# A two-layer encoder on one core: the output product in eight pieces, its weights chunk by chunk, two PSUM banks for transposed weights and three for scores, x and result on two queues

## The reference

```
diff heads (8): s = einsum('mbhqd,mbhkd->mbhqk', q, k) * scale + bias      # two maps m of 512 keys
                a = softmax(s);  w = a[0] - lam * a[1]
                o = rms_norm(w @ v, norm_g) * (1 - lam_init)
near heads (8): s = q @ k_window * scale + bias (masked);  o = softmax(s) @ v_window   # 256 keys
h = concat(o_diff, o_na) @ w_out                    # (512 x 1024) @ (1024 x 1024)
x = layer_norm(alpha * x + h, ln1_g, ln1_b)
f = PEER(x)                                         # routing, 16384 experts, 8 heads x top 16
x = layer_norm(alpha * x + f, ln2_g, ln2_b)
```

## Time and profile before

| | us |
|---|---|
| timed executions (3) | 3433.43, 3438.35, 3439.59 |
| median | 3438.35 |
| the profiled execution's own time | 3430.17 |
| its span, first to last instruction | 3428.4 |
| setup, to the first instruction of project | 0 to 19.1 |
| attend of the first layer | 172 to 402 |
| attend of the second layer | 1870 to 2102 |
| from the last vector instruction to the end | 3410.0 to 3428.4 |

### The profile page before, as it was taken

The page is one execution under the profiler, slowest core; times in us unless marked ns, Lnnn a source line. Parts: engine busy times, 40 slices in busy tenths (PEclk is TensorE's granted clock), DMA queues, the critical chain, the costliest instruction groups (busy, mean ns, idle before and its releaser), DMA issues. The chain is left out here.

```text
span 3428.4 us, 48751 instructions
## 1 busy us (share of the span) xinstructions
PE 3166.2 (92%) x16726; PEld 2801.7 (82%) x16726; DVE 2477.6 (72%) x5112; ACT 1233.9 (36%) x1756; POOL 1086.5 (32%) x684
## 2 busy tenths in 40 slices
PE   7978799899899999999889787998999999999996
PEld 6855489899899999988677555898988999999885
DVE  3165298899688888778732563898986888787786
ACT  2355233344333333333323552333443333332332
POOL 0030046500255545433200200573003555454331
PEclk9989899999999999999989998999999999999998
DMA  7541224455899999889675312243649999898995
GB/s 256 139 126 38 100 82 158 156 205 214 332 341 351 336 330 338 322 307 350 223 267 126 105 56 91 91 169 137 237 196 364 349 351 341 317 339 289 335 355 185
DMA packets 334536, 806.11 MB, mean 235 GB/s; under 512 B 38928, under 2 KB 195088, under 8 KB 299824
## 3 DMA queue, kind: packets, MB, share of 16 engines
q1 hardware_dynamic: 258576, 527.41, 44.9%
q0 software_dynamic: 73728, 268.47, 20.9%
q10 hardware_dynamic: 2080, 8.39, 0.6%
HBM read 711.38 MB, written 99.09 MB: 236 GB/s over the span
## 5 line engine op out<-in xcount | busy, mean ns | idle before, releaser
L183 POOL DMA_INDIRECT g_ring<-in_peer_u,g_idx x256 | 363.1, 1418 | 797.7 <-DVE g_ring L193 747.1
L246 PE MATMUL o_bank<-v_hi,w_hi 128*128 128x512 f32 x1536 | 599.5, 390 | 15.6 <-DVE w_lo L1631 15.6
L247 PE MATMUL o_bank<-v_lo,w_hi 128*128 128x512 f32 x1536 | 600.4, 391 | 0.0
L248 PE MATMUL o_bank<-v_hi,w_lo 128*128 128x512 f32 x1536 | 600.3, 391 | 0.0
L183 POOL DMA_INDIRECT g_ring<-in_peer_v,g_idx x256 | 373.9, 1460 | 502.3 <-DVE x_sb L201 449.8
L246 PE MATMUL h_bank<-x_hi,ws_hi 128*128 128x384 f32 x1152 | 385.7, 335 | 4.5 <-PEq L1299 4.5
L248 PE MATMUL h_bank<-x_hi,ws_lo 128*128 128x384 f32 x1152 | 385.7, 335 | 0.0
L247 PE MATMUL h_bank<-x_lo,ws_hi 128*128 128x384 f32 x1152 | 385.3, 334 | 0.0
L1551 ACT CAST v_hi<-v_raw 128x2048 fp32r<-128x2048 f32 x128 | 244.9, 1913 | 388.0 <-PE o_bank L248 343.2
L1616 DVE TENSOR_TENSOR v_lo<-v_raw,v_hi 128x2048 fp32r<-128x2048 f32 x128 | 293.0, 2289 | 125.4 <-ACT v_hi L1551 125.2
L193 DVE SCALAR_TENSOR_TENSOR g_ring<-g_ring,x_sb 128x1024 f32<-128x1024 f32 x256 | 306.2, 1222 | 94.7 <-DMA g_ring<-in_peer_u,g_idx 92.8
(11 more groups left out here) (197 smaller groups left out, 6043.7 us busy)
## 6 DMA issues: line engine op xcount, KB each, us to landing
ws_raw<-in_uT SPq DMA_DIRECT2D x128, 1024.0 KB
v_raw<-in_peer_v SPq DMA_DIRECT2D x128, 1024.0 KB
gates_T<-gate_stage SPq DMA_DIRECT2D x12, 4096.0 KB, 12.7
g_raw<-gates_T SPq DMA_DIRECT2D x128, 384.0 KB
w_raw<-in_w_in SPq DMA_DIRECT2D x24, 1024.0 KB, 9.3
ws_raw<-hidden_T SPq DMA_DIRECT2D x56, 384.0 KB
w_out_half<-in_w_out SPq DMA_DIRECT2D x8, 2048.0 KB, 8.2
ws_raw<-in_peer_wq SPq DMA_DIRECT2D x16, 1024.0 KB
```

The costliest lines, as they stand in the source:

```text
L183: nc.gpsimd.indirect_dma_start(out=tail.ring[n % RING][:, :], out_offset=None, in_=table.rearrange("l e d -> (l e) d"), in_offset=bass.Ind ...
L246: nc.tensor.matmul(out, lh, rh, start=start, stop=False)
L247: nc.tensor.matmul(out, lh, rl, start=False, stop=False)
L248: return nc.tensor.matmul(out, ll, rh, start=False, stop=stop)
```

## The change

Seven edits:

1. The eight loads of x are split: four on SP (partitions 0 to 63) and four on ACT (64 to 127). The stores at the end likewise.
2. `Tb` becomes two banks used in turn. `turn(u)` now waits for `move(u - 2)`, not `move(u - 1)`.
3. `SB` goes from 4 to 3, which pays for it in PSUM (8 banks in all).
4. The output product is eight pieces of two matmuls (`mul_0` to `mul_7`) in slots 24 to 27 and 29 to 32. It was four pieces of four matmuls in slots 25, 26, 29 and 30.
5. w_out's half is loaded in four chunks of 512 KB with a semaphore each. A piece waits for its own chunk, and SP loads the next half's chunk n as soon as piece n of the first half is done.
6. The first load of w_out (with the layer norm's parameters) moves on SP from before unit 0 to unit 8, and so behind the first three groups of the next tile's queries.
7. ACT's `turn_diff` moves from slot 25 to 24, and DVE's `add_1` from 32 to 33.

```diff
@@ setup
             for tt in range(TT):
-                for g in range(TB):
-                    sp.dma_start(per["x"][block_rows(g), tt, :], column_tokens(a["x"], tt, g)).then_inc(x_in, 16)
+                sp.dma_start(per["x"][block_rows(0), tt, :], column_tokens(a["x"], tt, 0)).then_inc(x_in, 16)
...
+        @block.scalar
+        def _(act):
+            for tt in range(TT):
+                nc.scalar.dma_start(per["x"][block_rows(1), tt, :], column_tokens(a["x"], tt, 1)).then_inc(x_in, 16)
@@ attend
-        SB = 4
+        SB = 3
         S = [m.bank(f"S{i}") for i in range(SB)]
-        Tb, Hb = m.bank("Tb"), m.bank("Hb")
+        Tb, Hb = [m.bank(f"Tb{i}") for i in range(2)], m.bank("Hb")
...
-        PE_SLOTS = {"turn_na": 20, "turn_diff": 23, "mul_0": 25, "mul_1": 26, "mul_2": 29, "mul_3": 30}
-        ACT_SLOTS = {"square": 18, "turn_na": 21, "turn_diff": 25, "spread": 33}
+        PIECES = 4
+        WO_AT = 8
+        MULS = {f"mul_{n}": u for n, u in enumerate((24, 25, 26, 27, 29, 30, 31, 32))}
+        PE_SLOTS = {"turn_na": 20, "turn_diff": 23, **MULS}
+        ACT_SLOTS = {"square": 18, "turn_na": 21, "turn_diff": 24, "spread": 33}
...
-        SP_SLOTS = {"mul_1": 26}
+        SP_SLOTS = {f"mul_{n}": MULS[f"mul_{n}"] for n in range(PIECES)}
@@ attend, SP
+                if u == WO_AT:
+                    sp.wait_ge(nb_ready, NNH + 2)
+                    for n in range(PIECES):
+                        load_wo(wo, half(0, 0), wo_in[n], 2 * n, 2)
+                    sp.dma_start(lnp[:, 0, :], at(a["ln1_g"], l * D, [[0, P], [1, D]])).then_inc(ln_in, 16)
+                    sp.dma_start(lnp[:, 1, :], at(a["ln1_b"], l * D, [[0, P], [1, D]])).then_inc(ln_in, 16)
             def tail(qt, piece):
-                if piece == "mul_1" and qt + 1 < TT:
-                    sp.wait_ge(hid, 2 * qt + 1)
-                    load_wo(wo[:, :, :], half(qt, 1))
+                n = int(piece[-1])
+                if qt + 1 < TT:
+                    sp.wait_ge(hid, 2 * PIECES * qt + n + 1)
+                    load_wo(wo, half(qt, 1), wo_in[n], 2 * n, 2)
...
-            sp.wait_ge(nb_ready, NNH + 2)
-            load_wo(wo[:, :, :], half(0, 0))
@@ attend, PE
-                if u >= 1:
-                    pe.wait_ge(moved, u)
+                if u >= 2:
+                    pe.wait_ge(moved, u - 1)
...
-                        pe.wait_ge(wo_in, 16 * (qt + i + 1))
+                        pe.wait_ge(wo_in[part], 16 * (qt + i + 1))
...
-                    for c in range(4 * part, 4 * part + 4):
+                    for c in (2 * part, 2 * part + 1):
...
-                    if part == 1:
-                        ins.then_inc(hid, 1)
+                    ins.then_inc(hid, 1)
@@ store
-                for g in range(TB):
-                    sp.dma_start(column_tokens(out, tt, g), per["x"][block_rows(g), tt, :]).then_inc(written, 16)
+                sp.dma_start(column_tokens(out, tt, 0), per["x"][block_rows(0), tt, :]).then_inc(written, 16)
+        @block.scalar
+        def _(act):
+            for tt in range(TT):
+                nc.scalar.dma_start(column_tokens(out, tt, 1), per["x"][block_rows(1), tt, :]).then_inc(written, 16)
```

More of the change, by code:

```diff
@@ L602, in attend @@
         rs = m.sb("ln_rs", [P, 2])
-        SB = 4
+        SB = 3
         S = [m.bank(f"S{i}") for i in range(SB)]
-        Tb, Hb = m.bank("Tb"), m.bank("Hb")
+        Tb, Hb = [m.bank(f"Tb{i}") for i in range(2)], m.bank("Hb")
         O = [m.bank(f"O{i}") for i in range(2)]
         wo_end_in = sem("a_wo_end")
-        wo_in, ln_in, placed = sem("a_wo"), sem("a_ln_in"), sem("a_placed")
+        ln_in, placed = sem("a_ln_in"), sem("a_placed")
+        wo_in = [sem(f"a_wo{n}") for n in range(4)]
         qd_in = [sem(f"a_qd_in{g}") for g in range(NDH // 2)]
@@ L624, in attend @@
         AHEAD, BEHIND = 3, 2
-        PE_SLOTS = {"turn_na": 20, "turn_diff": 23, "mul_0": 25, "mul_1": 26, "mul_2": 29, "mul_3": 30}
-        ACT_SLOTS = {"square": 18, "turn_na": 21, "turn_diff": 25, "spread": 33}
-        DVE_SLOTS = {"read_diff": 18, "read_na": 19, "sums": 20, "gain": 22, "add_0": 28, "add_1": 32, "spread": 35,
+        PIECES = 4
[3 more added lines that the diff above has]
+        ACT_SLOTS = {"square": 18, "turn_na": 21, "turn_diff": 24, "spread": 33}
+        DVE_SLOTS = {"read_diff": 18, "read_na": 19, "sums": 20, "gain": 22, "add_0": 28, "add_1": 33, "spread": 35,
                      "norm": 37}
         POOL_SLOTS = {"sums": 20, "spread": 35}
-        SP_SLOTS = {"mul_1": 26}
+        SP_SLOTS = {f"mul_{n}": MULS[f"mul_{n}"] for n in range(PIECES)}
         def head(u):
@@ L672, in load_q, with load_wo @@
                                  parts(parts_scratch, b // 2, 0, 4 * g, 4, qt * P, P)).then_inc(qd_in[g], 16)
-            def load_wo(dst, i, landed=wo_in):
-                sp.dma_start(dst, at(a["w_out"], l * (D * D) + i * (D // 2), [[D, P], [P * D, DC], [1, D // 2]]))\
-                    .then_inc(landed, 16)
+            def load_wo(dst, i, landed, first, count):
+                src = at(a["w_out"], l * (D * D) + i * (D // 2) + first * (P * D), [[D, P], [P * D, count], [1, D // 2]])
+                sp.dma_start(dst[:, first:first + count, :], src).then_inc(landed, 16)
             def unit(u):
@@ L686, in unit @@
                         sp.wait_ge(maxed, before + n)
-                        load_wo(wo_end, half(TT - 1, 1), wo_end_in)
+                        load_wo(wo_end, half(TT - 1, 1), wo_end_in, 0, DC)
+                if u == WO_AT:
[4 more added lines that the diff above has]
+                    sp.dma_start(lnp[:, 1, :], at(a["ln1_b"], l * D, [[0, P], [1, D]])).then_inc(ln_in, 16)
             def tail(qt, piece):
-                if piece == "mul_1" and qt + 1 < TT:
-                    sp.wait_ge(hid, 2 * qt + 1)
-                    load_wo(wo[:, :, :], half(qt, 1))
+                n = int(piece[-1])
+                if qt + 1 < TT:
+                    sp.wait_ge(hid, 2 * PIECES * qt + n + 1)
+                    load_wo(wo, half(qt, 1), wo_in[n], 2 * n, 2)
             for g in range(NDH // 2):
@@ L768, in move @@
                 n = chunks(u)
-                nc.scalar.copy(wT[u % 2][:, 0:n, :].rearrange("p a b -> p (a b)"), Tb[:, 0:n * P]).then_inc(moved, 1)
+                nc.scalar.copy(wT[u % 2][:, 0:n, :].rearrange("p a b -> p (a b)"), Tb[u % 2][:, 0:n * P]).then_inc(moved, 1)
             def unit(u):
@@ L872, in tail @@
                     f = half(qt, i)
-                    dve.wait_ge(hid, 2 * qt + i + 1)
+                    dve.wait_ge(hid, PIECES * (2 * qt + i + 1))
                     xs = x[:, qt, f * 512:(f + 1) * 512]
@@ L973, in tail @@
                     ins.then_inc(cat_turned, 1)
-                if piece in ("mul_0", "mul_1", "mul_2", "mul_3"):
-                    i, part = divmod(int(piece[-1]), 2)
-                    if (qt, i) == (TT - 1, 1):
+                if piece in MULS:
+                    i, part = divmod(int(piece[-1]), PIECES)
+                    end = (qt, i) == (TT - 1, 1)
+                    w = wo_end if end else wo
+                    if end:
                         pe.wait_ge(wo_end_in, 16)
                     else:
-                        pe.wait_ge(wo_in, 16 * (qt + i + 1))
+                        pe.wait_ge(wo_in[part], 16 * (qt + i + 1))
                     if i == 0:
```

7 lines of the change are left out of this document (3 added, 4 removed).

## The result

| | before | after |
|---|---|---|
| median of the timed executions, us | 3437.94 (4, 3433.43 to 3439.59) | 3392.32 (4, 3386.24 to 3396.41) |
| ratio | | 0.9875, 95% interval 0.9853 to 0.9896 |
| the profiled execution's own time | 3430.17 | 3396.41 |

The change takes 45.6 us off the median; 51 were forecast.

The account below looks back on a forecast made before the run. No engine is full; attend is bound by engines waiting for each other. Terms 22.4 + 28.1 + 0 + 0.5 = 51 us off the median 3438.4 give 3387 us; its own range 3377 to 3399, the overall range 3370 to 3409.

Parts of the forecast that it names:

- The queries' stop: PE's stop for the second tile's queries goes in both attends, with the slow clock behind it: 22.4 us off.
- The waits for w_out: PE's three waits per attend for w_out's next half go, with the slow clock behind each: 28.1 us off.
- the forecast tile: A tile's period in an attend falls from 50.8 us to 45.5 to 46.2 us.
- The second `Tb` and three banks: In the attends, second `Tb` and one score bank fewer cancel: 0, bounds 37 us off to 44 us on.
- The start: Leading six diff heads of each attend's first tile: three score banks cost 1.5 us per attend.
- `add_1`: Behind a tile's last output piece, DVE has less lead and PE waits about 1.3 us.
- rival C: PE's scores wait behind each diff-head map, over 25 us of `rowmax` waits an attend; slower, 3475 us; chance 0.04.
- PEclk near 0.97, attend 205 to 207 us: Sign of being right: attends of 205 to 207 us, not 230 and 232, PE's granted clock nearer 0.97.
- Two queues: Load of x and store: second queue only adds an issuer, DMA share stays near 0.5; 0.5 us off.

Follow-up runs that it names:

- the fourth bank: The changed kernel with both adds one slot later, plus `Hb` as a fourth score bank in the first tile: 3373.9 us, ratio 0.9805.

## Why the prediction was right, step by step

The number was right, 3387 against 3392, and most steps were. Some sizes were off, and part of the agreement is luck.

- **The queries' stop, 22.4 us.** Right. Units 12 to 16 are 10.3 and 10.9 us shorter in the profiles (units 12 to 24 together 22.9), and the edit alone gives 18 to 23 us.
- **The waits for w_out, 28.1 us.** Right in cause: without the chunks 28 to 33 us come back, with the wait at its old place. The size was too high: from unit 24 on the two attends together gain 21.4 us, and the forecast tile of 45.5 to 46.2 us became 46.8 and 46.4. (A chunk has five units before its use, slots 24 and 29, not the four of the working.)
- **The second `Tb` and three banks, together nothing.** Near for the old order of pieces (5 us), where what the banks win is waited away at w_out. But it was said of the new order too, and there the pair is worth 33 us. The working took PE's stretch as one that doesn't wait. It would: with one `Tb` PE waits 29.6 us for the copy in the new order, where the old one has 19.0. The traces show two causes, both of the change's own making: the early adds, which the working saw in part, and ACT's `turn_diff`, which edit 7 puts ahead of the copy and for which the working has no term. So the second bank fends off a loss that the rest of the change would have brought.
- **The start, 1.5 us an attend.** The mechanism was named and under-sized, and the sum put it at nothing. It is 4.2 and 4.4 us in this profile, at a clock of 0.73 in units 0 to 8 and 0.81 in 8 to 12. The eight attends of four other kernels with three banks there (the bank trade alone, w_out in one load, late adds, `add_0` alone late) take 31.7 to 33.2 us up to unit 12, against 30.3 and 30.1 before, so 1.5 to 3 us are nearer to the banks' own price.
- **`add_1`, 1.3 us a tile.** Measured 1.9 (4.85 less 2.98), and the larger one was missed: `add_0` waits for `mul_3`, PE waits behind it, three times an attend. The new wait of scores for the maxima is 15.1 us, not 10, and below the 25 that would have meant rival C. Moving both adds gives 17 us.
- **PEclk near 0.97, attend 205 to 207 us.** The clock was wrong: 0.91 and 0.90. The low clock at the start of an attend and in its last product stays, over a stretch that is 18 us shorter. The 207.6 us look like a hit, but the 205 to 207 were set against windows of 230 and 232 us, which are longer than the attend; between the same marks it is 225.3 and 225.7 to 207.6.
- **Two queues, 0.5 us.** Right as a sum (ratio 1.0000), wrong as a picture: 2.5 us off the load and about 1.5 on the store. The share stayed at one half, as read. The Trainium skill says in "DMA: Bandwidth & Descriptors" (section on issuing engines not being separate DMA queues) that starting DMAs from several engines saves only the time to start them. The share of 0.52 agrees with that. The rate in the load does not: over 9 to 13 us it is 192 to 211 GB/s in the ten profiles with two queues and 132 to 177 in the three with one, and here the measurement decides.

**Where luck came in.** By the profiles the attends gave 36 us, some 15 short of the 50.5 forecast for them: 8.6 us are the starts, put at nothing, and 6.7 the shortfall from unit 24 on. By the medians the whole change gave 45.6. The 8.2 us by which before's median stands above its profiled execution were carried over as a constant. They are not one. The profile with two queues has before's attends and needs 7.9 us more for them, with the clock at 0.60 to 0.73 in the places named above. The 49 executions of the kernel before that ran beside the experiments say the same: the five fastest (3429.0 to 3430.4 us) have a mean granted clock of 0.966 to 0.968, the six slowest (3447.1 to 3450.8) one of 0.960 to 0.962. The profiles of the new order don't have these places. Against the profiles the 51 us forecast met 33.8, and it is the medians that made up 12 of the missing 17 us, for which the working has no term. That the new order is what rid the kernel of them is inferred from which profiles have them; no run isolates it.

## What to carry to other kernels

An instruction that waits for a distant producer also holds back what is queued behind it on its engine: before trading away a buffer, look at what stands behind each such wait and who needs it, and try the waiting instruction one slot later. Moving two adds by one slot gave 17 us of 3392, with numbers in three slot tables changed. A part that is worth little alone (5 us for the banks) can be worth 33 in the changed schedule, so the worth of parts is measured by undoing them as well as by doing them alone. And a loss that shows when one part is undone may be the doing of another: look in the trace for which instruction now stands ahead (here ACT's `turn_diff`) before the loss is called the bank's.

## What was not expected of the hardware

- The granted clock isn't the same in two executions of the same attends. Right behind the DVE-bound stretch of a tile (15 to 19 us in which PE was busy about 7 tenths of the time) it is 0.58 to 0.73 in some profiles and 1.00 in others, and the low one costs up to 3 us each time.
- A gain in front of such a place can be taken back by it: in one attend 2.9 us were won in the leading heads and 4.5 lost behind them at 0.69, and of six attends with the fourth bank three kept the gain.
- With two queues on the same half of the DMA engines' time, the mean packet of 4 KB in the load of x took 182 ns and not 225 (180 to 206 ns in the ten profiles with two queues, 202 to 244 in the three with one). The store didn't gain (199 ns and 196).
